# Delta stage: lane groups of 2, 3, 4, 4, 3 steps in place of 2, 4, 4, 4, 2, the second one loaded earlier, and two masked scores ahead of GpSimd's columns

## The reference, cut to what matters

```python
def _gated_delta_rule(q, k, v, g, beta):
    # S_t = exp(g_t) S_{t-1} (I - beta_t k_t k_t^T) + beta_t k_t v_t^T,  o_t = S_t^T q_t
    ...
    lower = jnp.where(strict, jnp.einsum('bnhid,bnhjd->bnhij', k_beta, kc) * decay, 0.0)
    a_mat = lower + jnp.eye(C, dtype=lower.dtype)
    sol = lax.linalg.triangular_solve(a_mat, rhs, left_side=True, lower=True, unit_diagonal=True)
    ...
    def step(state, inp):
        v_new = u_i - jnp.einsum('bhcd,bhde->bhce', w_i, state)
        o_i = q_i * exp(g_i) @ state + a_i @ v_new
        state = state * exp(g_last) + k_dec^T @ v_new
```

## Time and profile before

| what | value |
|---|---|
| three runs | 4226.88, 4220.05, 4225.28 us; median 4225.28 us |
| the profiled execution | 4225.21 us, span of its trace 4223.4 us |
| PE, DVE, ACT, POOL busy | 91%, 69%, 42%, 22% of the span |
| delta stage of the first layer | from about 742 us to 1166 us of the trace |
| delta stage of the second layer | from about 2806 us to 3231 us |

### The profile page before, as it was taken

How to read it: one execution, slowest core, us unless ns; L and a number is a source line. 1 busy time by engine, 2 the same in 40 slices (tenths; PEclk the granted TensorE clock), 3 DMA queues, 4 the chain that set the end, 5 groups by cost and what they waited for, 6 DMA issues and landing times. The chain is left out here.

```text
span 4223.4 us, 56010 instructions
## 1 busy us (share of the span) xinstructions
PE 3841.1 (91%) x19078; PEld 3016.1 (71%) x19078; DVE 2933.6 (69%) x3425; ACT 1789.3 (42%) x2511; POOL 934.0 (22%) x816
## 2 busy tenths in 40 slices
PE   4999997689989999998899999966997999999896
PEld 3877776589957766766778777755996677767674
DVE  4686255566779999985257843836766999999743
ACT  3111011345557777772131101122553777777511
POOL 0054510487500000000002544026953000000000
PEclk9999998889989999999999999987998999999997
DMA  6111154544540000005331112744454300000345
GB/s 254 75 62 60 76 186 158 157 118 137 142 164 23 23 24 25 21 14 177 115 130 61 61 71 96 245 131 109 139 154 129 114 25 21 25 24 21 82 148 224
DMA packets 338080, 424.58 MB, mean 101 GB/s; under 512 B 106128, under 2 KB 255760, under 8 KB 315480
## 3 DMA queue, kind: packets, MB, share of 16 engines
q1 hardware_dynamic: 335032, 401.45, 29.6%
q10 hardware_dynamic: 2880, 20.97, 1.2%
HBM read 274.09 MB, written 148.05 MB: 100 GB/s over the span
## 5 line engine op out<-in xcount | busy, mean ns | idle before, releaser
L1801 DVE TENSOR_REDUCE att_sb_part<-att_banks 128x1 f32<-128x512 f32 x992 | 680.7, 687 | 100.3 <-PE att_banks L1686 86.4
L1788 ACT ACTIVATE att_sb_probs<-att_banks 128x1024 f32<-128x1024 f32 x512 | 525.0, 1025 | 311.0 <-PE att_banks L1714 310.8
L1819 DVE TENSOR_TENSOR att_sb_p_lo<-att_sb_probs,att_sb_p_hi 128x1024 fp32r<-128x1024 f32 x512 | 622.5, 1216 | 18.8 <-ACT att_sb_p_hi L1792 18.8
L1792 ACT ACTIVATE att_sb_p_hi<-att_sb_probs 128x1024 fp32r<-128x1024 f32 x512 | 544.5, 1063 | 16.1
L357 PE MATMUL proj_banks<-proj_sb_h_hi,proj_sb_w_hi 128*128 128x512 f32 x1600 | 506.4, 398 | 31.9 <-DVE proj_sb_pad L507 26.6
L357 PE MATMUL proj_banks<-proj_sb_h_lo,proj_sb_w_hi 128*128 128x512 f32 x1600 | 503.4, 396 | 0.0
L357 PE MATMUL proj_banks<-proj_sb_h_hi,proj_sb_w_low 128*128 128x512 f32 x1600 | 502.6, 396 | 0.0
L414 POOL TENSOR_TENSOR proj_sb_high_squares<-proj_sb_out 128x2048 fp32r<-128x2048 f32 x28 | 100.9, 3603 | 1598.2 <-ACT proj_sb_out L453 1278.8
L1095 PE MATMUL dn_banks<-dn_sb_room 128*128 128x128 f32 x3072 | 381.1, 284 | 61.3 <-DMA dn_sb_room<-proj 27.0
L1095 PEld LDWEIGHTS dn_banks<-dn_sb_room 128*128 128x128 f32 x3072 | 369.2, 199 | 83.5 <-DMA dn_sb_room<-proj 37.3
L1714 PE MATMUL att_banks<-att_sb_q,att_sb_k 68*128 68x512 f32 x1024 | 409.1, 400 | 0.0
(11 more groups left out here) (229 smaller groups left out, 5735.2 us busy)
## 6 DMA issues: line engine op xcount, KB each, us to landing
proj<-proj_sb_out SPq DMA_DIRECT2D x40, 1024.0 KB, 3.8
dn_sb_kq<-proj SPq DMA_DIRECT2D x64, 512.0 KB, 4.9
proj_sb_w_raw<-in_w_in SPq DMA_DIRECT2D x52, 536.0 KB, 3.7
dn_sb_room<-proj SPq DMA_DIRECT2D x32, 768.0 KB, 5.0
proj_sb_x<-x_res SPq DMA_DIRECT2D x16, 1024.0 KB, 12.1
att_sb_q<-att_q SPq DMA_DIRECT2D x64, 256.0 KB, 2.6
ahead_delta<-x_res SPq DMA_DIRECT2D x16, 1024.0 KB, 6.5
x_res<-ahead_delta SPq DMA_DIRECT2D x16, 1024.0 KB, 4.2
```

Source lines behind the costliest of these rows:

```text
L1788: nc.scalar.activation(probs[:, pair % 2], ps[:, 2 * (pair % 2):2 * (pair % 2) + 2, :], ACT.Exp, scale=SCALE).then_inc(s["exp_done"], 1)
L1792: nc.scalar.activation(p_hi[:, pair % SLOTS], probs[:, pair % 2], ACT.Copy).then_inc(s["hi_done"], 1)
L1801: nc.vector.tensor_reduce(part[:, w // NQ, w % NQ:w % NQ + 1], ps[:, 4 + w % 2, :], AX.X, ALU.max) \
L1819: nc.vector.tensor_tensor(p_lo[:, pair % SLOTS], probs[:, pair % 2], p_hi[:, pair % SLOTS].bitcast(F32), ALU.subtract).then_inc(s["lo_done ...
```

## The change

It touches five places in `delta_net`. The groups get 2, 3, 4, 4, 3 steps. `load_lanes(1)`, which now needs ten chunks, goes from chunk 12 to chunk 10 of SP's loop, and `prepare_lanes(1)` from behind chunk 13 to behind chunk 12 of DVE's. On POOL the masked scores of step 0 go from behind group 1's columns into the local loop, and those of step 1 from behind the ten columns of step 0 to ahead of them. `SCAN_COLS`, `PREPARED`, `SCALED`, `STORED` and `LANES_IN` stay.

```diff
-GROUP_STEPS = [(0, 2), (2, 6), (6, 10), (10, 14), (14, 16)]
-GROUP_READY = [4, 12, 16]
+GROUP_STEPS = [(0, 2), (2, 5), (5, 9), (9, 13), (13, 16)]
+GROUP_READY = [4, 10, 16]
...
                     if n == 4:
                         load_lanes(0)
+                    if n == 10:
+                        load_lanes(1)
                     if n == 12:
-                        load_lanes(1)
                         load_kq(0)
...
+                    if n == 8:
+                        pool.wait_ge(s["att"], N_DIR)
+                        for side in SIDES:
+                            masked_scores(side, 0)
                 eliminate(1, 0, COLS)
                 pool.wait_ge(s["att"], NC)
-                for side in SIDES:
-                    masked_scores(side, 0)
                 done = [0] * len(GROUP_STEPS)
                 for j in range(NC):
+                    if j == 0:
+                        for side in SIDES:
+                            masked_scores(side, 1)
...
-                    if j + 1 < NC:
+                    if 0 < j < NC - 1:
                         for side in SIDES:
                             masked_scores(side, j + 1)
...
-                    if n == 13:
+                    if n == 12:
                         prepare_lanes(1)
```

## The result

The change makes the kernel a little slower. In the first comparison the median was 4236.73 us (9 runs, 4228.51 to 4242.71) against 4226.88 us (9 runs), a ratio of 1.0024, 95% interval 1.0013 to 1.0034. The same two kernels were compared twice more: 1.0013 (1.0003 to 1.0023) and 1.0018 (1.0008 to 1.0027). So the cost is 5.5 to 10 us. The forecast was 4230 us, with a range of 4221 to 4236: the sign is right, all three intervals lie above 1, and the first median lies 0.7 us outside the range.

What follows compares the result with a forecast made beforehand. The prediction took POOL's unbroken chain of columns in the delta stage as the bound. Against 4225.21 us it added 2.3 + 1.6 + 2 x 0.5 = 4.9, so 4230 us, with a range of 4221 to 4236.

Steps and rivals of the forecast that it cites:

- The mechanism: POOL's chain sets when step 8 begins; its last column of step 7 comes 2.3 and 1.6 us later.
- How the numbers follow: Closing step that set the time from the first case, bounds 4222 and 4233, and the range 4221 to 4236.
- the forecast's own case: POOL's chain sets the end, standing still costs a little more than its early start wins: 4226 to 4233, chance 0.68.
- The early lane load: DVE's idle time for the lane load goes, so POOL's first column comes 3.70 and 4.43 us earlier.
- Behind group 1: Before step 1's first column, POOL stands still about 10 us for `output(0)` and saves the old pair's 4.11 us.
- Contention goes with the pair: With step 0's masked scores moved away, `scale_lanes(1)` on DVE takes 3.30 us instead of 5.15.
- The clock: Step 0's first `solve` on PE runs fast, as idle time ahead of it falls to about 1 us.
- the rival of the slow clock: PE's clock stays low through step 0: 4.65 us on top, 4234.8; chance 0.19 together with contention that stays.
- Who waits where: DVE waits for POOL's columns three times a layer, some 2, 3 and 6 us, last at step 7's end.
- The end of step 7: PE idles longer there and more of step 8 runs at the lower clock: 0 to 1 us a layer, 0.5 taken.
- The early start: Rival: the scan keeps its early start, needing 7 us and more of POOL reserve behind step 1; 4208.7, chance 0.08.
- The lane load was in by chunk 12: Rival said it is not in by then and DVE waits there: 8.1 us on top, 4238; chance 0.05.

Runs made afterwards that it cites:

- Scores 1 back: The changed kernel with the masked scores of step 1 at their old place behind step 0's ten columns; ratio to before 0.9968, once more 0.9969.
- Lanes only: The changed kernel with both pairs of masked scores at their old places, leaving the new groups and the earlier lane load; ratio to before 0.9991.
- scores 0 only: The kernel before with only the masked scores of step 0 moved into the local phase; ratio to before 0.9981.

## Why the prediction was right or wrong

The terms, as means per layer over the three traces of each kernel (six stages each), in us (within one kernel the first piece varies by up to 4.0 us, the second and the last by up to 1.3, the two from group 1's columns to step 1's first column by 0.2 at most):

| piece of the stage | forecast | measured |
|---|---|---|
| start to the seventh chunk's products | 0 | +0.6 |
| from there to POOL's first column | -4.1 | -3.5 |
| group 1's columns | 0 | +0.3 |
| to step 1's first column | +6.0 | +6.4 |
| from there to POOL's last column | 0 | -0.7 |
| last column to the end of the stage | +0.5 | +0.3 |
| sum (two layers: twice) | +2.4 | +3.4 |

**The mechanism was right.** POOL's chain sets the end, its standing still costs more than the early start wins, and the last column comes late: in the first layer 281.04 us after the start of the stage, where it was 278.45 (2.6 later, forecast 2.3), in the second 280.95 against 279.72 (1.2, forecast 1.6). In the mean of six stages each it is 3.1 us later, of which 0.6 come about ahead of anything that was changed. Scores 1 back shows the cause alone: without that edit the stages are 21.3 us shorter (865.28 - 843.95), some 10.7 a layer, with an idle time of 10.3 in the traces.

**The step that failed is "How the numbers follow".** The range was made of the bounds of the change's own terms, around the one profiled execution. It had no term for how far one comparison of this kernel lies from another, though the sum itself says that a measurement can't tell 8.5 us from nothing: the same code, compared with itself, came out at 1.0007 and at 0.9997, the stages' starts differ by up to 4.8 us, and what lies outside of the stages by 15 us in thirteen traces. The forecast of 4.9 us stands against 6.9 in the traces, with the three of before spread over 4.2 us and the three of the changed kernel over 3.0; of the 6.9, 1.2 (0.6 a layer) come about ahead of the seventh chunk, where nothing is changed, so 5.7 are left. The first comparison gave 9.9 us, the other two 1.0013 and 1.0018, which are 5.5 and 7.6 us of 4227. In the first pair of traces the spans differ by 10.2 us, 6.0 in the stages and 4.2 outside of them. And 1.7 us are the kernel before itself, more than the 0.7 by which the range was missed: the sum starts from 4225.21 us, and in the comparison the median of before was 4226.88. The later two medians of the changed kernel, 4235.21 and 4234.55 us, lie inside the range, but above the 4226 to 4233 of the forecast's own case.

**Terms that were mis-sized.** The early lane load won 3.5 us, not 4.1: I took the waits of one trace (3.70 and 4.43), and in the three traces of before they were 3.89 in the mean; the other 0.4 I can't put down to a row. Behind group 1 it is 6.4 instead of 6.0, of which 0.2 is idle time (10.32 and 10.31, where 10.10 was worked out). The columns took 0.7 less from step 1 on. In both kernels the same `prepare_lanes` and `scale_lanes` of DVE fall into this stretch and slow a few of POOL's instructions there, but other ones: before, `scale_lanes(3)` at the end of step 5 met a pair of masked scores in the first layer (4.13 us instead of 2.51), after it met columns. No single row gives the 0.7, and why the sum is smaller isn't shown.

**Contention goes with the pair.** Right: `scale_lanes(1)` takes 3.17 us from start to end. Lanes only against scores 1 back shows it to be the pair's doing. By SBUF — State Buffer of the Trainium skill, in SBUF: two separate sides, the two engines lock a port pair that they share, and by that rule the pair is free once POOL is silent. The traces agree: 5.08 us in lanes only, where the masked scores began first (875.14 against 875.21), and 3.17 in the changed kernel, where POOL is silent. In scores 1 back POOL isn't silent, and there it is POOL's column that takes longer, as in scores 0 only, while DVE needs 3.20 us.

**The clock.** Right in its result, and not for my reason. I had expected some 1 us of idle time ahead of the first solve and a fast clock for it. The idle time was 2.85 us, as long as before (2.78), and the clock was 1.00 all the same. I had moved only the solve: PE's work ahead of it came earlier as well and ended at 872.5 instead of 877.8. So the rival of the slow clock fell, but the reason that I gave against it, that the idle time is gone, didn't hold. In the six stages of the changed kernel the idle time ahead of the first solve was 1.11 to 2.85 us, and the solve took 2.19 us each time; in the six of before the idle time was 2.15 to 3.10 us, and the solve took 3.33 to 3.78. What gave the fast clock is open, and as a forecast it was luck.

**Who waits where.** DVE waits for POOL twice in a layer, 3.10 and 7.05 us, and not three times. The wait at `scale_lanes(2)` didn't come: at 927.46 there is none, since PE had already given 2.2 us of its lead to step 2's blocks and 1.5 to the clock behind them. I had looked for a stall over blocks in step 4, where PE waits for none longer than 0.7 us, and not in step 1, where the group's store and its load stand close behind each other. It cost nothing, as all of it lies under the wait at the end of step 7. In step 5 PE waits 1.51 us for the masked scores, as forecast.

**The end of step 7** was +0.3 a layer, inside my 0 to 1. In one trace alone it looked like 1.0 and 1.2 us; the piece takes values from 149.5 to 152.2 us in all kernels, and even with six stages of each, 0.3 isn't told from nothing.

**The rivals.** The early start was not kept, as POOL has no reserve. The lane load was in by chunk 12 (no idle time at 822.29).

## What to carry to other kernels

Ahead of an in-order chain that sets the end, a moved instruction costs the whole time until its operands are there, however short it is itself: 2.5 us of masked scores cost some 10.7 us a layer here, and the same edits without it made the kernel 0.3% faster. Look at a change of several edits edit by edit, because the useful ones can hide behind a costly one. And before a range is set, ask how far two comparisons of the same code lie apart: here the interval of one comparison is some 4 us to either side, about as large as the effect that was forecast.

## What the runs showed of the hardware

- The same idle time doesn't give the same clock. PE began sixteen matmuls after 2.85 us of idle time and they took 2.19 us (clock 1.00); after 2.78 us they had taken 3.60 (clock 0.52); after 4.20 and 3.36 us they took 3.78 and 3.59, after 2.50 us 3.17, after 0.91 and 1.94 us 2.05. What PE did ahead of the idle time differed too. The work in front of the first solve, before (released at 867.51) and after (at 863.52):

```profile
867.51 3.78 PE L1095 MATMUL dn_banks<-dn_sb_room 128*128 128x128 f32 x16 [8.27 <-DVE dn_sb_room L1460]
871.08 4.96 PE L1095 MATMUL dn_banks<-dn_sb_state,dn_sb_kq 128*128 128x128 f32 x32
875.88 1.95 PE L1095 MATMUL dn_banks<-c_sq_acc,dn_sb_w 128*128 128x128 f32 x16
```

```profile
863.52 3.61 PE L1096 MATMUL dn_banks<-dn_sb_room 128*128 128x128 f32 x16 [9.30 <-DVE dn_sb_room L1466]
866.96 3.74 PE L1096 MATMUL dn_banks<-dn_sb_state,dn_sb_kq 128*128 128x128 f32 x32
870.53 1.95 PE L1096 MATMUL dn_banks<-c_sq_acc,dn_sb_w 128*128 128x128 f32 x16
```

The thirty-two matmuls take 3.74 us after (clock 1.00) and 4.96 before (clock 0.74 from 871.08 to 876.00). Whether this decides the clock behind the idle time, the runs don't separate.
- DVE and POOL block each other by the instruction. DVE's two `scale_lanes` instructions take 2.90 + 2.14 us beside masked scores that began 0.07 us earlier (lanes only), and 1.95 + 1.22 beside columns that began later; then POOL's two column instructions take 0.82 + 1.23 us instead of 0.25 + 0.27 (scores 0 only), and each ends about 0.1 us behind the DVE instruction that began ahead of it (876.69 against 876.61, 878.00 against 877.87).
- On SP the issue of two loads of keys and queries took 6.98 us behind the stores of the group's blocks, and the four loads of blocks behind them 4.89 us, where such four take 1.80 later in the scan. It was so in the kernel before as well (6.62 and 5.20 us). The timeline of SP after, first layer:

```profile
879.23 6.98 SPq L993 DMA_DIRECT2D dn_sb_kq<-proj  x2
886.32 4.89 SPq L1001 DMA_DIRECT2D c_sq_acc<-d_blk  x4
...
927.61 1.80 SPq L1001 DMA_DIRECT2D c_sq_acc<-d_blk  x4
```

It is these blocks that PE waits for in step 1 (894.27). Moving the one load behind the other shortened PE's wait (2.50 to 0.91 us), but I haven't shown what holds SP there.
